# One stage for the attention's finish, the convolutions, the output projection and the second norm of a two-layer hybrid diffusion kernel

## The chip, the cores and the metric

The program runs on one core of one Trainium2 chip, in fp32 throughout. The metric is the device time of one execution in microseconds, as the median of several runs. A core has a matrix engine (TensorE, PE in the rows; its weight loads are PEld), a vector engine (DVE), an activation engine (ACT), GpSimd (POOL), and SyncE (SP), which here only starts transfers. The engines run apart from each other and meet at semaphores. Transfers issued by SP are rows named SPq.

## What is computed

Two layers over 1152 tokens of width 1024: 1024 latent tokens and 128 context tokens. The parts that the change touches are these (the rest is cut):

```python
def _trunk_layer(x, cond, p, ...):
    sh1, sc1, g1, sh2, sc2, g2 = silu(cond) @ w_mod + b_mod       # six rows of 1024, one set per token group
    h = rmsnorm(x, norm_g[0]) * (1 + sc1) + sh1
    z = h @ w_in                                                  # split among three head groups
    o_hg = hgrn(...)                                              # 256 columns
    o_da = rmsnorm(diff_attention(...), diff_subln_g) * (1 - lam_init)      # 4 heads x 128 columns
    zc = short_conv(z_hy, conv_w, conv_b); v, x1, x2 = split(zc)  # Hyena, 3 x 256 columns
    y = x1 * long_conv(v, filt[0]);  o_hy = x2 * long_conv(y, filt[1])
    mix = concat(o_hg, o_da, o_hy) @ w_out
    x = x + g1 * mix
    h2 = rmsnorm(x, norm_g[1]) * (1 + sc2) + sh2
    x = x + g2 * expert_choice_ffn(h2)                            # 16 experts, router on h2
```

## The kernel before

The program is a sequence of stages, each a block in which every engine has its own written-out instruction list. The order within an engine is the order of the code; nothing reorders it. `stage` (L70) opens a block with its own semaphores. At its end all engines meet, SP clears each of the stage's semaphores with one instruction (L83), and all engines meet again (L84) before anything of the next stage starts. Transfers of a stage are therefore issued only after that.

The stages are: `prologue` (L2423), and then for each of the two layers `modulate_and_filter` (L1058), `norm_to_channels` (L87), `project_and_recur` (L219), `attention` (L842), `hyena_and_finish` (L1357), `project_out_and_norm` (L1738) and `route_and_experts` (L1909), and at last `epilogue`.

`prologue` copies the whole input x (4.7 MB) into an internal DRAM tensor `x_rows`, and loads six small constants. The last of these (`select_e`) is issued only when the copy has landed, and the SiLU on ACT waits for all six.

`modulate_and_filter` multiplies the condition by `w_mod` in 12 blocks of 512 columns. `modulate(b)` leaves 4 partial rows in PSUM, ACT keeps them, and `turn(b)` sums and turns them into columns (four pairs of passes of 2 columns each, L1119). Between the blocks PE makes 20 filter spectra of the convolutions, which DVE takes out of PSUM in order (`take`, L1299) into a buffer that SP stores to DRAM (L1107, L1108, L1110). SP's queue carries the `w_mod` blocks and the DFT tables first, then these stores.

`hyena_and_finish` begins with SP loading z0 (the first of six 128-channel blocks of the convolution's input), four small vectors, four DFT units, z1, z2, four more units, z3, z4 and the rest. DVE: `short(0)`, `short(1)` (short convolution of a block; L1590, L1594, L1598), `finish_attention` (row sums of squares L1606, root, scaling of 128x4608 values L1612), `short(2)`, `short(3)`, then `products` and `result` for two orders and two halves `ct`. ACT: the square of the whole attention output (L1559), `centre(1)` (L1540, centre tap of block 1), `take_in(0)` (L1546, L1549, token rows out of PSUM), `centre(2)`, the root, `centre(3)`, `take_in(1)` and so on. PE: `turn_in(0)` (9 transposes, L1422), `forward(0,0)` (L1458, 64 products in 128 passes with 8 DFT units), `turn_in(1)`, `forward(0,1)` with the attention's transposes between, `inverse(0,0)` (L1478), `ctx_forward` (L1497), `inverse(0,1)`, and the same for order 1, ending with `inverse(1,1)`. DVE then does `result(1,1)` (L1661, L1664).

`project_out_and_norm` begins with SP loading `w_out` in two halves of 2 MB (L1751), the router weights (L1752) and the first three token tiles of x (L1758). Meanwhile DVE makes 16 diagonal matrices of the gate g1 (`gate_rows`, L1727), PE multiplies them by ones (L1734) and ACT copies the 2 x 1024 gate rows out of PSUM (L1883). Then for each of 9 token tiles t: PE makes 16 products of 512 columns (32 passes, L1812); DVE multiplies by the gate (L1844) and adds x (L1848); ACT squares (L1890); the norm's row follows; PE transposes the tile before it (L1776), and ACT and DVE shape h. Tile t+1's products are queued on PE ahead of tile t's transposes.

## Time and profile before

| | |
|---|---|
| median of 3 runs | 4454.81 us (4450.07 to 4462.17) |
| the profiled execution | 4453.28 us, of it span 4451.5 us |
| mean granted TensorE clock | 0.951 of full speed |
| PE busy | 3987.0 us (90%), 24498 passes |
| DVE, ACT, POOL busy | 1689.1, 1057.1, 160.3 us |
| DMA | 666.12 MB, mean 150 GB/s |

The span is from the first to the last instruction; the execution's own time is 1.8 us longer. A product in fp32 is two passes on PE, so the rows count passes. PE is busy 90% of the span, but shares of busy time say little here, since the stages follow one another and each has its own limit. What a change in one stage gives is read from the instruction that ends last in it, and from the idle time before the next stage's first instruction.

### The profile page before, as it was taken

How to read it: one execution, taken by the hardware profiler on the slowest of the kernel's cores; microseconds unless marked ns; L12 is line 12 of the kernel's file. 1: busy time of each engine (PE TensorE's matmuls, PEld its weight loads, DVE VectorE, ACT ScalarE, POOL GpSimd, SP SyncE). 2: the span in 40 equal slices, each digit the busy share in tenths (PEclk: the TensorE clock that was granted, in tenths of full speed). 3: DMA queues.
4: the chain of work that ended last, by engine and by line, in shares of the span. 5: the costliest groups of instructions: out<-in, count | busy, mean ns of one | idle time of the engine just before them, and what ended most of it. 6: DMA issues, size and time to landing. Idle time of an engine off the chain costs nothing. (4 is left out here: it accounts for less than half of the span.)

```text
span 4451.5 us, 57780 instructions
## 1 busy us (share of the span) xinstructions
PE 3987.0 (90%) x24498; PEld 3176.2 (71%) x24498; DVE 1689.1 (38%) x2954; ACT 1057.1 (24%) x2386; POOL 160.3 (4%) x96
## 2 busy tenths in 40 slices
PE   6899999787894999999887999988889869999996
PEld 2456885575544999999834668856665369999995
DVE  3335752677535111111142368327774341111111
ACT  1252211673011111111112522117720101111112
POOL 0000002000000000000000000010000000000000
PEclk9899999998996999999988999999989889999998
DMA  6511120103124887788455011210032257787774
GB/s 229 208 37 47 38 68 31 48 1 117 68 90 177 288 283 257 278 284 286 139 205 193 29 56 39 80 54 4 1 117 96 104 214 270 274 288 276 264 273 177
DMA packets 321775, 666.12 MB, mean 150 GB/s; under 512 B 21966, under 2 KB 60494, under 8 KB 319376
## 3 DMA queue, kind: packets, MB, share of 16 engines
q1 hardware_dynamic: 309712, 619.44, 38.3%
q0 software_dynamic: 9216, 33.56, 3.2%
q10 hardware_dynamic: 2592, 9.44, 0.5%
q8 instruction: 195, 3.19, 0.3%
q14 instruction: 60, 0.49, 0.0%
HBM read 596.34 MB, written 70.78 MB: 150 GB/s over the span
## 5 line engine op out<-in xcount | busy, mean ns | idle before, releaser
L2024 PE MATMUL ps<-arena 128*128 128x144 f32 x8192 | 1014.9, 287 | 10.3 <-DVE arena L2184 10.3
L2024 PEld LDWEIGHTS ps<-arena 128*128 128x128 f32 x8192 | 1008.0, 190 | 17.9 <-DVE arena L2184 17.9
L384 PE MATMUL ps<-arena 128*128 128x384 f32 x1920 | 631.0, 490 | 9.4 <-PEq L84 9.4
L384 PEld LDWEIGHTS ps<-arena 128*128 128x128 f32 x1920 | 365.5, 192 | 258.8 <-issue 15.3
L2048 PE MATMUL ps<-arena 128*128 128x144 f32 x4096 | 507.1, 286 | 0.0
L2048 PEld LDWEIGHTS ps<-arena 128*128 128x128 f32 x4096 | 503.6, 190 | 0.0
L2195 DVE TENSOR_TENSOR arena<-arena,ps 128x144 f32<-128x144 f32 x256 | 77.9, 304 | 920.1 <-ACT arena L2100 920.1
L2100 ACT ACTIVATE arena<-ps 128x144 f32<-128x144 f32 x256 | 74.3, 290 | 1011.7 <-PE ps L2024 1011.7
L1812 PE MATMUL ps<-arena 128*128 128x512 f32 x576 | 252.3, 597 | 5.7 <-DMA arena<-in_w_out 5.7
L381 PE MATMUL ps<-arena 128*128 128x256 f32 x1152 | 256.0, 380 | 0.0
L2184 DVE TENSOR_SCALAR arena<-ps,mod 128x128 f32<-128x128 f32 x256 | 87.1, 403 | 435.5 <-PE ps L2004 435.5
L526 ACT ACTIVATE arena<-ps 128x384 f32<-128x384 f32 (+1 forms) x192 | 86.1, 449 | 691.5 <-PE ps L384 463.9
L381 PEld LDWEIGHTS ps<-arena 128*128 128x128 f32 x1152 | 216.5, 191 | 28.4
L2107 ACT ACTIVATE arena<-ps,mod 128x128 f32<-128x128 f32 (+1 forms) x512 | 136.0, 317 | 386.6 <-PE ps L2048 386.6
L1009 ACT ACTIVATE arena<-ps,arena 128x768 f32<-128x768 f32 (+2 forms) x272 | 205.4, 767 | 31.2 <-DVE arena L973 28.9
L1812 PEld LDWEIGHTS ps<-arena 128*128 128x128 f32 x576 | 108.7, 191 | 139.8 <-issue 137.6
L889 PE MATMUL ps<-arena 64*128 64x256 f32 (+2 forms) x1056 | 169.7, 461 | 26.3 <-PEq L84 18.4
L429 PEld LDWEIGHTS ps<-arena 128*128 128x128 f32 x1296 | 158.2, 198 | 29.5 <-issue 23.6
L429 PE MATMUL ps<-arena 128*128 128x128 f32 x1296 | 159.8, 281 | 21.8 <-DVE arena L761 20.8
L938 PE MATMUL ps<-arena 128*128 128x128 f32 x1296 | 169.8, 278 | 1.8 <-ACT arena L1021 1.6
L938 PEld LDWEIGHTS ps<-arena 128*128 128x128 f32 x1296 | 157.3, 194 | 3.4 <-ACT arena L1021 3.1
L918 PE MATMUL ps<-ident,arena 128*128 128x128 f32 x648 | 110.5, 284 | 53.7 <-DVE arena L989 50.2
(307 smaller groups left out, 3887.9 us busy)
## 6 DMA issues: line engine op xcount, KB each, us to landing
arena<-in_w_gate SPq DMA_DIRECT2D x64, 2048.0 KB, 7.9
arena<-in_w_up SPq DMA_DIRECT2D x64, 2048.0 KB, 14.0
arena<-in_w_down SPq DMA_DIRECT2D x64, 2048.0 KB, 12.3
arena<-in_w_mod SPq DMA_DIRECT2D x24, 2048.0 KB, 15.1
arena<-in_w_in SPq DMA_DIRECT2D x28, 1024.0 KB, 5.3
arena<-in_dft_units SPq DMA_DIRECT2D x48, 512.0 KB, 7.2
arena<-x_rows SPq DMA_DIRECT2D x47, 512.0 KB, 6.2
x_rows<-arena ACTq DMA_DIRECT2D x18, 512.0 KB, 2.6
```

The lines of the kernel that those rows point to most:

```text
L381: last = nc.tensor.matmul(m.ps[:, at:at + 256], m.hT[:, k, q * P:(q + 1) * P], m.Wr[:, slot % 2, k, :], start=(k == 0), stop=(k == KD - 1))
L384: last = nc.tensor.matmul(m.ps[:, at:at + TC], m.Wr[:, slot % 2, k, jj * P:(jj + 1) * P], m.hT[:, k, q * TC:(q + 1) * TC], start=(k == 0), ...
L429: last = nc.tensor.matmul(m.ps[:, at:at + P], keys[:, ch * P:(ch + 1) * P], m.xq[:, n % 2, ch].rearrange("p hh t -> p (hh t)"), start=keys ...
L889: last = nc.tensor.matmul(banks[:, mp, col:col + keys.shape[1]], m.aqk[r, h, qt * P:(qt + 1) * P], keys[r], start=True, stop=True)
L918: last = nc.tensor.transpose(m.ps[:, 3072 + k * P:3072 + (k + 1) * P], m.prob[:, n % 2, 0, j * P:(j + 1) * P], m.ident[:, :])
L938: last = nc.tensor.matmul(m.ps[:, 3584:3584 + DV], m.aT[:, n % 2, j, :], v, start=(j == 0), stop=(j == nk - 1))
L1009: nc.scalar.activation(m.prob[:, n % 2, mp, a:b], banks[:, mp, 0:b - a], ACT.Exp, bias=m.nmax[:, n, mp:mp + 1], accum_out=m.sums[:, n, int ...
L1812: last = nc.tensor.matmul(m.ps[:, at:at + 512], m.oT[:, k, t * P:(t + 1) * P], m.wo[:, k, h * 512:(h + 1) * 512], start=(k == 0), stop=(k ...
L2024: last = nc.tensor.matmul(m.ps[:, at:at + CAP], m.wbuf[:, 2 * h + which, k, q * P:(q + 1) * P], m.xe[:, e % 2, k, :], start=(k == 0), stop ...
L2048: last = nc.tensor.matmul(m.ps[:, at:at + CAP], m.wbuf[:, 4 + h, k, q * P:(q + 1) * P], m.hid[:, k, :], start=(k == 0), stop=(k == KD - 1))
L2107: last = nc.scalar.activation(m.yT[:, n, a:b], m.ps[:, at + a:at + b], ACT.Copy, scale=m.mod[:, 5 * KD + n, g:g + 1])
L2184: last = nc.vector.tensor_scalar(m.xe[:, e % 2, k, 0:CAP_L], m.ps[:, 3072 + k * P:3072 + (k + 1) * P], m.mod[:, 4 * KD + k, 0:1], m.mod[:, ...
```

## The change

The stages `hyena_and_finish` and `project_out_and_norm` become one, `mix_and_norm`. The attention stage loads z0 to z2 and the four small vectors (with one new semaphore). In the merged stage ACT's square stands behind `take_in(0)`. SP issues the two halves of `w_out` once all forward transforms are through, into the place of the forward DFT units; the gate rows and three tiles of x follow once all products are through. PE starts tile 0 of the projection with 14 of its 16 products right behind `inverse(1,1)`; the last two wait for `result(1,1)`. `gate_rows` is gone. In its place the modulation stage turns blocks 4 and 5, which hold g1, with one product of 16 x 512 each, DVE adds the bias to 2 x 512 values twice, and SP stores the rows to DRAM (four new semaphores). The input x is no longer copied: layer 0 reads it where it lies.

```diff
--- before.py
+++ after.py
...
-                sp.dma_start(xbuf[:, t], m.x_dram[t * P:(t + 1) * P, :]).then_inc(s[f"x_loaded{t}"], 16)
+                sp.dma_start(xbuf[:, t], m.x_in(l)[t * P:(t + 1) * P, :]).then_inc(s[f"x_loaded{t}"], 16)
...
+            for j in range(3):
+                sp.dma_start(m.z[j], m.zhy_dram[j * P:(j + 1) * P, :]).then_inc(s["z_loaded"], 16)
+            for dst, src in ((m.hy_cw, "hy_conv_w"), (m.hy_cb, "hy_conv_b"), (m.hy_skip, "hy_skip"),
+                             (m.sub_gain, "diff_subln_col")):
+                sp.dma_start(dst[:, :], m.d[src][l]).then_inc(s["z_loaded"], 16)
             sp.wait_ge(s["spectra_loaded"], 80)
+            sp.wait_ge(s["z_loaded"], 112)
...
+            sp.wait_ge(s["w_used"], 8)
+            sp.dma_start(m.gate_bias[:, :], m.d["gate_bias"][l]).then_inc(s["gate_bias"], 16)
+            sp.wait_ge(s["gate_rows"], 2)
+            for i in range(2):
+                sp.dma_start(m.gate_dram[:, i * PC:(i + 1) * PC], m.gate_rows[32 * i:32 * i + 2, :])\
+                    .then_inc(s["gate_stored"], 16)
...
+            sp.wait_ge(s["gate_stored"], 32)
...
+                if b in GATE_BLOCKS:
+                    i = 32 * (b - GATE_BLOCKS[0])
+                    if i == 0:
+                        pe.wait_ge(s["sums_read"], 1)
+                    nc.tensor.matmul(m.ps[i:i + E, 2560:3072], m.select_e[:, :], m.mod_rows[:, b % 2, :], start=True,
+                                     stop=True).then_inc(s["turned"], 1)
+                    return
...
+                if src == 2560:
+                    dve.sem_inc(s["sums_read"], 1)
...
+            dve.wait_ge(s["gate_bias"], 16)
+            dve.wait_ge(s["turned"], 6)
+            for i in range(2):
+                r = slice(32 * i, 32 * i + 2)
+                nc.vector.tensor_tensor(m.gate_rows[r, :], m.ps[r, 2560:3072], m.gate_bias[r, :], ALU.add)\
+                    .then_inc(s["gate_rows"], 1)
...
-def hyena_and_finish(nc, m, l):
+def mix_and_norm(nc, m, l):
...
-            load_z(0)
-            for dst, src in ((m.hy_cw, "hy_conv_w"), (m.hy_cb, "hy_conv_b"), (m.hy_skip, "hy_skip"),
-                             (m.sub_gain, "diff_subln_col")):
-                sp.dma_start(dst[:, :], m.d[src][l]).then_inc(s["w_loaded"], 16)
...
-            load_z(1)
-            load_z(2)
...
+            sp.wait_ge(s["forward"], 8)
+            w = m.d["w_out"][l].rearrange("(k p) (h n) -> h p k n", p=P, n=512)
+            for h in range(2):
+                sp.dma_start(m.wo[:, :, h * 512:(h + 1) * 512], w[h]).then_inc(s[f"w_loaded{h}"], 16)
+            sp.wait_ge(s["spectra"], 8)
+            for g in range(2):
+                sp.dma_start(m.gbo[:, g], m.gate_dram[g].partition_broadcast(P)).then_inc(s["gate_loaded"], 16)
...
+                    if t == 3:
+                        sp.wait_ge(s["result"], 8)
+                        sp.dma_start(m.wr[:, :, :], m.d["w_router"][l]).then_inc(s["router_loaded"], 16)
...
+            for t in range(NT):
+                if t >= 2:
+                    pe.wait_ge(s["scaled"], t - 1)
+                if t == 0:
+                    pe.wait_ge(s["result"], 6)
+                    for h in range(2):
+                        pe.wait_ge(s[f"w_loaded{h}"], 16)
+                        project(t, h, range(KD - 1))
+                    pe.wait_ge(s["result"], 8)
+                if t == 1:
+                    pe.wait_ge(s["ctx_result"], 8)
+                for h in range(2):
+                    last = project(t, h, range(KD) if t else range(KD - 1, KD))
+                last.then_inc(s["projected"], 1)
...
-            nc.scalar.activation(sq, m.o_att.rearrange("p c v -> p (c v)"), ACT.Square).then_inc(s["square"], 1)
-            act.wait_ge(s["w_loaded"], 64)
             centre(1)
             take_in(0)
+            nc.scalar.activation(sq, m.o_att.rearrange("p c v -> p (c v)"), ACT.Square).then_inc(s["square"], 1)
...
-                    dve.wait_ge(s["z0"], 16)
...
-            dve.wait_ge(s["w_loaded"], 64)
...
-def gate_rows(nc, m, block_engines, s, which):
...
-def project_out_and_norm(nc, m, l):
...
-            gate_rows(nc, m, (dve, None), s, 0)
-            dve.wait_ge(s["rows_ready"], 1)
+            dve.wait_ge(s["gate_loaded"], 32)
...
-            act.wait_ge(s["diag_used"], 16)
-            nc.scalar.activation(m.gbo.rearrange("p g n -> p (g n)"), m.ps[:, 2048:4096], ACT.Copy)\
-                .then_inc(s["rows_ready"], 1)
...
-        m.wo = view(m.R_W, KD, D)
-        m.xr = view(9216, 3, D)
-        m.dx = view(12288, 2, D)
...
+        m.wo = view(38656, KD, D)
+        m.xr = view(25088, 3, D)
+        m.dx = view(28160, 2, D)
...
-        m.gbo = view(19456, 2, D)
+        m.gbo = view(47908, 2, D)
...
+        m.x_in = lambda l: m.x_dram if l else d["x"]
+        m.gate_dram = nc.dram_tensor("mix_gate", (2, D), F32, kind="Internal").ap()
...
-            hyena_and_finish(nc, m, l)
-            project_out_and_norm(nc, m, l)
+            mix_and_norm(nc, m, l)
...
-    with stage(nc, m, "loaded", "copied", "silu") as (block, s):
+    with stage(nc, m, "loaded") as (block, s):
         @block.sync
         def _(sp):
-            sp.dma_start(m.x_dram, m.d["x"]).then_inc(s["copied"], 16)
             sp.dma_start(m.cond[:, :, :], m.d["cond"]).then_inc(s["loaded"], 16)
             sp.dma_start(m.row_number[:, :], m.d["row_number"]).then_inc(s["loaded"], 16)
             sp.dma_start(m.ident[:, :], m.d["ident"]).then_inc(s["loaded"], 16)
             sp.dma_start(m.select[:, :], m.d["select"]).then_inc(s["loaded"], 16)
             sp.dma_start(m.alt[:, :], m.d["alt"]).then_inc(s["loaded"], 16)
-            sp.wait_ge(s["copied"], 16)
             sp.dma_start(m.select_e[:, :], m.d["select_e"]).then_inc(s["loaded"], 16)
             sp.wait_ge(s["loaded"], 96)
```

The first place is the start of the stage on ACT, in layer 0. The 128x4608 row is the attention's square, the 128x1152 rows are `centre`, and 128x8x128 with 128x128 is `take_in(0)`. Before:

```order
L1559 ACTIVATE arena<-arena 128x4608
L1540 ACTIVATE arena<-arena,hy_cb,hy_cw 128x1152
L1546 ACTIVATE arena<-ps 128x8x128
L1549 ACTIVATE arena<-ps 128x128
L1540 ACTIVATE arena<-arena,hy_cb,hy_cw 128x1152
L1565 ACT_TABLE_LOAD
L1565 ACTIVATE small<-small 128x36
```

After:

```order
L1657 ACTIVATE arena<-arena,hy_cb,hy_cw 128x1152
L1663 ACTIVATE arena<-ps 128x8x128
L1666 ACTIVATE arena<-ps 128x128
L1678 ACTIVATE arena<-arena 128x4608
L1657 ACTIVATE arena<-arena,hy_cb,hy_cw 128x1152
L1681 ACT_TABLE_LOAD
L1681 ACTIVATE small<-small 128x36
```

The square has moved from the first place to the fourth, behind the two copies that release PE's first transform; the root (128x36) keeps its place.

The second place is PE at the seam of the two old stages, layer 0: the last inverse transforms, the gate rows (`ones`), and the projection (128x512 of L1812). Here rows count products, not passes. Before:

```order
L1506 MATMUL ps<-arena 128x128 x4
L1478 MATMUL ps<-arena 128x512 x16
L76 UNCONDITIONAL_BRANCH
L1766 UNCONDITIONAL_BRANCH
L1734 MATMUL ps<-arena,ones 128x128 x16
L1812 MATMUL ps<-arena 128x512 x32
L1776 MATMUL ps<-ident,arena 128x128 x8
```

After:

```order
L1557 MATMUL ps<-arena 128x128 x4
L1529 MATMUL ps<-arena 128x512 x16
L1623 MATMUL ps<-arena 128x512 x32
L1594 MATMUL ps<-ident,arena 128x128 x8
```

The two branches (the end of one stage and the start of the next) and the 16 products with `ones` are gone, and the projection's 32 products of tiles 0 and 1 stand directly behind the last inverse.

The third place is SP around the old seam. Before, with the 48 semaphore clears between the stages (ISA) and the 29 at the second stage's end further down:

```order
L1412 DMA arena<-in_dft_units 128x1024 x8
L1390 DMA arena<-z_hyena 128x1152
L76 UNCONDITIONAL_BRANCH
L83 ISA x48
L1747 UNCONDITIONAL_BRANCH
L1751 DMA arena<-in_w_out 128x8x512 x2
L1752 DMA arena<-in_w_router 128x256
...
L83 ISA x29
```

After, with the clears of the merged stage at its end:

```order
L1440 DMA arena<-in_dft_units 128x1024 x8
L1424 DMA arena<-z_hyena 128x1152
L1446 DMA arena<-in_w_out 128x8x512 x2
L1449 DMA arena<-mix_gate 128x1024 x2
L1458 DMA arena<-in_x 128x1024 x3
...
L1454 DMA arena<-in_w_router 128x256
...
L83 ISA x71
```

The loads of `w_out` now stand behind the last convolution input in the same queue, and 48 + 29 clears at two ends have become 71 at one. The same count is 34 before and 38 after at the modulation stage's end, 13 and 14 at the attention's, and 3 and 1 at the prologue's.

## Rows read from the trace of the kernel before

**Rows 1.** Timeline of the prologue: start, length, engine, line; then idle time before.

```profile
0.74 0.65 SPq L2428 DMA_DIRECT2D x_rows<-in_x  x1
...
3.90 0.49 SPq L2433 DMA_DIRECT2D alt_sb<-in_alt  x1
17.76 0.33 SPq L2435 DMA_DIRECT2D select_e_sb<-in_select_e  x1
...
20.36 0.37 SPq L1075 DMA_DIRECT2D arena<-in_pos_all  x1
```

**Rows 2.** Landing of the four small vectors (L1395), layer 0.

```profile
DMA to landing us min/median/max: 2.7/3.1/3.6
```

**Rows 3.** Timeline of the convolution stage's start, layer 0.

```profile
1027.59 4.04 ACT L1559 ACTIVATE arena<-arena 128x4608 f32<-128x4608 f32 x1 [1.24 <-PEq L84]
...
1033.03 0.88 DVE L1590 TENSOR_SCALAR arena<-arena,hy_cw,hy_cb 128x1152 f32<-128x1152 f32 x1 [8.85 <-DMA sub_gain<-in_diff_subln_col]
...
1037.13 2.19 PE L1422 MATMUL ps<-ident,arena 128*128 128x128 f32 x9 [11.19 <-DVE arena L1598]
...
1040.98 1.00 ACT L1546 ACTIVATE arena<-ps 128x1024 f32<-128x1024 f32 x1
...
1042.04 1.34 ACT L1540 ACTIVATE arena<-arena,hy_cb,hy_cw 128x1152 f32<-128x1152 f32 x1
...
1042.25 17.41 PE L1458 MATMUL ps<-arena 128*128 128x128 f32 x128 [2.93 <-ACT arena L1546]
...
1044.15 4.94 DVE L1606 TENSOR_REDUCE small<-arena 128x36 f32<-128x4608 f32 x1
```

**Rows 4.** The same stage, later: PE waits for DVE; a later forward transform.

```profile
1100.07 2.07 PE L1497 MATMUL ps<-arena 128*128 128x256 f32 x4 [2.76 <-DVE arena L1652]
...
1119.28 14.56 PE L1458 MATMUL ps<-arena 128*128 128x128 f32 x128 [1.11 <-ACT arena L1555]
```

**Rows 5.** Busy time in one stretch; last three: granted clock, DMA share, GB/s.

```profile
1034.00:1036.00 2.00, 0.00 (x0) 0.00 (x0) 1.97 (x3) 0.00 (x0) 0.00 (x0) 0.50 1.01 397
```

**Rows 6.** The convolution stage's start, layer 1.

```profile
3229.11 4.04 ACT L1559 ACTIVATE arena<-arena 128x4608 f32<-128x4608 f32 x1 [1.22 <-PEq L84]
...
3245.61 4.95 DVE L1606 TENSOR_REDUCE small<-arena 128x36 f32<-128x4608 f32 x1
```

**Rows 7.** Timeline of the seam, layer 0, and one steady tile.

```profile
1182.10 1.28 DVE L1661 SCALAR_TENSOR_TENSOR arena<-arena,hy_sk,ps 128x1024 f32<-128x1024 f32 x1 [4.67 <-PE ps L1478]
...
1188.23 1.01 SPq L1751 DMA_DIRECT2D arena<-in_w_out  x2
...
1197.57 29.40 PE L1812 MATMUL ps<-arena 128*128 128x512 f32 x64 [3.67 <-DMA arena<-in_w_out]
...
1213.35 1.22 DVE L1844 TENSOR_TENSOR arena<-ps,arena 128x1024 f32<-128x1024 f32 x1 [20.03 <-PE ps L1812]
...
1227.68 13.90 PE L1812 MATMUL ps<-arena 128*128 128x512 f32 x32
```

**Rows 8.** The seam, layer 1.

```profile
3383.63 1.28 DVE L1661 SCALAR_TENSOR_TENSOR arena<-arena,hy_sk,ps 128x1024 f32<-128x1024 f32 x1 [4.67 <-PE ps L1478]
...
3411.37 1.22 DVE L1844 TENSOR_TENSOR arena<-ps,arena 128x1024 f32<-128x1024 f32 x1 [16.73 <-PE ps L1812]
```

**Rows 9.** The semaphore clears of L83 between 1180 and 1200 us.

```profile
L83 SPq EVENT_SEMAPHORE_RANGE_CLEAR  x48: 25/25/31, 1184.9 to 1187.9; - x48
```

**Rows 10.** Timeline of the modulation stage's last part, layer 0.

```profile
151.45 1.06 SPq L1090 DMA_DIRECT2D arena<-in_w_mod  x2
...
163.53 0.95 PE L1119 MATMUL ps<-select_sb,arena 128*128 128x2 f32 x8
...
170.00 0.69 DVE L1299 TENSOR_TENSOR arena<-ps,arena 128x512 f32<-128x512 f32 x1 [5.58 <-PE ps L1200]
...
190.77 0.32 SPq L1110 DMA_DIRECT2D filter_spectra<-arena  x1
```

**Rows 11.** Landing of the last two `w_mod` loads (L1090), layer 0.

```profile
DMA to landing us min/median/max: 9.5/11.9/14.4
```

More of the change, by code:

```diff
@@ L1065, in modulate_and_filter @@
     G = KD // 4
-    with stage(nc, m, *(f"w_loaded{b}" for b in range(NBUF)), "w_used", "mod_small", "cond_ready", "rows_kept", "turned", "step",
+    GATE_BLOCKS = (4, 5)
+    with stage(nc, m, *(f"w_loaded{b}" for b in range(NBUF)), "w_used", "sums_read", "gate_bias", "gate_rows", "gate_stored", "mod_small", "cond_ready", "rows_kept", "turned", "step",
                "small_loaded", "decay_loaded", "biased", "hidden", "argued", "reduced", "sine", "taps_done", "taps",
@@ L1535, in _ @@
+            turn_x(NT - 1)
+            router(2)
+            turn_logits(2)
         @block.scalar
@@ L2401, in build @@
         m.ctx_table = view(51712, 2, CTX)
+        m.gate_bias, m.gate_rows = view(34304, 512), view(34816, 512)
         m.cond32 = view(51968, KD, 32)
```

245 lines of the change are left out of this document (105 added, 140 removed).

## The prediction

> **What bounds the kernel now.** I read the page's table by engine first, then the timeline at each place that the diff touches, and asked there which instruction ends last. PE is busy 90% of the span, so time can come only from stretches in which PE stands still, and there are three. The prologue: nothing computes until the copy of x has landed, since the last small load is issued behind it, at 17.76 us, and the next stage's first transfer goes out at 20.36 [rows 1]. The start of the convolution stage: ACT starts at 1027.59, but DVE only at 1033.03, when the small vectors and z0 are there, and PE at 1037.13 after 11.19 us idle [rows 3]. The seam: PE's last inverse releases DVE at 1182.10, and DVE gets the first projected tile at 1213.35, 31.25 us later, although a steady tile is 13.90 us of PE [rows 7]. In layer 1 the same stretch is 3383.63 to 3411.37, 27.74 us [rows 8]. Within the stages I look for who waits: at 1100.07 PE resumes after 2.76 us idle, released by DVE [rows 4], so up to there DVE's chain of products sets the time, and what the stage's start gives is what it gives DVE, not PE.
>
> **Prologue.** The copy's issue, the first on SP (at 0.74, 0.65 long), goes, and the small loads move up by about 0.7 us: `alt` from 3.90 to 3.2, and `select_e`, whose wait is gone, 0.5 behind it to 3.7. Before, from that issue to the next stage's first transfer were 20.36 - 17.76 = 2.60 us, landing, SiLU and clears included; kept, the next stage starts at 6.3, a gain of 14.1 [rows 1]. Six small loads now land together. The four small vectors, issued side by side behind one big load, took 2.7 to 3.6 us to land [rows 2], which would be up to 1.9 worse: 12.2. I take 13.6, near the first end, because here no big load is among them. Two clears fewer give 0.1, inside the rounding. From there layer 0's modulation runs as before, since its loads are issued by the start of the stage, and x is read later at the same size from another place.
>
> The Trainium skill ("DMA: Bandwidth & Descriptors", the anatomy of one DMA) gives a fixed part of about 2.0 us and a rate of 436 GB/s; for the 64 KB identity that is an estimate of 2.15 us, and the prologue's gain would be 13.6 to 13.7.
>
> **Start of the convolution stage.** z0, z1 and z2 (each 128x1152 values, 1.8 MB together) and the vectors come in during attention, a stage in which SP has only the spectra to load at its start; at 397 GB/s [rows 5] they are 4.5 us of transfer beside all of attention's compute. So DVE starts `short(0)` with the stage. From its start to PE's transposes were 1037.13 - 1033.03 = 4.10 us; the transposes take 2.19; `take_in(0)` on ACT 1042.04 - 1040.98 = 1.06; then the square, which stands there now, 4.04 [rows 3]. 4.10 + 2.19 + 1.06 + 4.04 and 0.1 of hand-overs are 11.5 us from stage start to DVE's row sums, where before it was 1044.15 - 1027.59 = 16.56. That is 5.05 us, and layer 1 repeats it: 3245.61 - 3229.11 = 16.50 [rows 6]. `short(1)` and `centre(1)` fit in before the square ends. PE's first transform starts 4.10 + 2.19 + (1042.25 - 1040.98) = 7.6 us into the stage, before 14.7, so PE gains 7.0, but 2 us of these turn into waiting for DVE: the idle of 2.76 [rows 4] becomes about 4.8. The move of the square is what makes the two differ. DVE sits idle some 4 us before the row sums now. The DFT units: z1 and z2 are no longer between them. At 397 GB/s [rows 5] one unit of 0.52 MB takes 1.3 us, and PE uses one in 17.41 / 8 = 2.2 us, the first only 7.6 us into the stage, so no transform waits. Gain 2 x 5.05 = 10.1.
>
> The clock is a loss here. The granted clock in rows 5 is 0.50, the lower level (1.2 GHz), after PE had been idle; the transform that began then took 17.41 us against 14.56 for the same work at full clock [rows 3, 4]. After the idle of 2.76 the four short passes took 2.07 us, at the lower level too. A longer idle may lengthen that stretch: from 0 (the 2.76 us row already paid) to 2.85 (the difference 17.41 - 14.56) per layer. I take 0.7, since the row at the same place is nearest: minus 1.4 in all. The Trainium skill ("TensorE: Matmul & The Clock Gate", why this matters for your kernels) says that an idle gap between bursts of matmuls drops PE to its lower clock and that sustained work brings it back. By that rule a gap that already drops the clock costs no more when it grows, and the sum would be 1.4 better.
>
> **The seam.** Gone are the 48 clears, which took 3.0 us from 1184.9 to 1187.9 [rows 9], the gate rows, ACT's copy, and the wait for `w_out`, which ended last in layer 0 at 1197.57 [rows 7]. After, PE goes from the last inverse straight into 28 of tile 0's 32 passes: 28 x 13.90 / 32 = 12.2 us. In that time DVE does `result(1,1)`, 2.5 us, so the last four passes do not wait. Tile 0 ends 13.9 us after the inverse. Gains: 31.25 - 13.9 = 17.35 and 27.74 - 13.9 = 13.85, together 31.2. The difference of the two was the clock and the landing, and neither is left. What could be late is `w_out`: SP issues it when the last forward transform is done, and two inverse transforms of 32 such passes, 27.8 us at least, lie between that and tile 0; 2 x 2 MB loads in another stage took up to 14.4 to land [rows 11]. Behind it in the queue stand the two gate loads of 0.5 MB and three tiles of x, 2.5 MB together, issued after DVE's last product, which the second half of the last inverse needs, so 7 us or more before its end, and needed 13.9 after it: 21 us for 6.3 us at 397 GB/s. Nothing waits. The router's weights come after `result(1,1)` and are read at tile 4, 60 us on.
>
> **What comes back.** The clears are serial: 3.0 / 48 = 0.0625 us each [rows 9]. The merged stage ends with 71 instead of 29, so 42 x 0.0625 = 2.6 us per layer, all on the path, 5.25 in all. Four more at each modulation stage and one at each attention stage: 10 x 0.0625 = 0.6.
>
> **Modulation.** On PE, block 4 and 5 are turned by 2 passes of 512 columns, 2 x 0.43 = 0.87 us, in place of 8 short ones of together 0.95 [rows 10]: nothing. `sums_read` is given right behind a row sum's reciprocal that DVE does before the first spectrum, and asked after the second lot of spectra. The two additions of 2x512 out of PSUM stand on DVE behind the take at 170.00 and cost about 0.7 each (the take of 128x512 is 0.69, a bound from above). Behind them are two tiny rows, the first `edge` and four more takes; DVE has slack until 190.77, where the last store is released by the last take [rows 10]. The first two stores go out 1.4 later, with some 19 us left to the last one's issue. The bias load is issued at 152.5, behind two `w_mod` loads that land at most 14.4 later, at 166.3 [rows 10, 11]; needed at 170.7. So the cost is nothing, from above bounded by 1.4 per layer if DVE's slack were gone, and not below nothing, since no work on PE goes.
>
> **The sum**, against the profiled execution: 13.6 + 10.1 - 1.4 + 31.2 - 5.25 - 0.6 = 47.65. 4453.28 - 47.65 = 4405.6 us. The median shown is 1.5 us above that execution, so I forecast 4406.
>
> **Rivals.** *A, the transfers take the place of the wait at the start.* Eight units go out at once when the stage opens. If the first transform ran at their pace, all of the 10.1 would be lost: 4416. Against it stands the 397 GB/s. *B, the seam gives only the clears and the gate rows.* If `w_out` lands so late that tile 0 still waits for it, as it does at 1197.57 in layer 0, the seam gives about half, 15.6: 4422. It needs a landing of over 28 us. *C, slower.* The bias load stands in one queue with the `w_mod` loads, and DVE waits for it in front of takes 16 to 19, which release PE's banks and the spectra's stores. If it lands at T after 170.7, DVE's slack is used up first (20 us to the last store's issue, less 5 of its own work and some 5 that the stores would come late: I take 10), then each us is lost twice, once per layer. Against a gain of 47.65 it decides from T = 170.7 + 10 + 24 = 205 us, 52 us after issue, against 14.4 seen; at 60 us (T = 212) it is 2 x 31 - 47.65 = 14 over, 4468. *D, the copy was hidden anyway*, that is, layer 0's modulation is bound by its `w_mod` stream from the first load on and only the start moves: the stream moves too, as it is issued by that start, so I give this little; it would cost 13.6: 4419. *E, the clock rule above*: 4404, inside my own range.
>
> **Chances.** Forecast with E 0.82 (4397 to 4413 alone: the prologue's 12.2 to 14.1, the clock's 0 to 5.7, about 3 us per start for where the clock rises, and the spread of the runs shown). A 0.06, B 0.03, D 0.04, C 0.02, nothing gained for another reason 0.03. The range goes from 4396 to 4420, which takes in A and D. A difference of 0.3%, 13.4 us, is about what a measurement of this kernel can tell from none. All cases but C and the last are faster by more: 0.95 faster, 0.03 within, 0.02 slower.
>
> **What would show it.** Right: the modulation stage's first transfer at 6 to 8 us; DVE's row sums 11 to 12 us after the stage's start, with ACT's square as their releaser; PE idle 4 to 6 us before the first context transform and DVE named for it; no idle on PE between the last inverse and tile 0, DVE's first gate multiplication 14 us after its `result(1,1)` starts; 71 clears over 4.4 us at the merged stage's end; DVE not waiting for a transfer behind take 15. Wrong: a wait for `in_w_out`, `in_dft_units` or `mix_gate` on any engine, PE at the lower clock in tile 0, or a first transform that starts later than 9 us into the stage.

## The result and the profile after

| | before | after |
|---|---|---|
| median | 4457.95 us (4450.07 to 4462.17, 4 runs) | 4408.41 us (4401.24 to 4408.75, 4 runs) |
| profiled execution | 4453.28 us, span 4451.5 | 4408.75 us, span 4407.0 |
| mean granted TensorE clock | 0.951 | 0.95 |

The ratio is 0.9889, with a 95% interval from 0.9876 to 0.9901. The forecast was 4406 us, inside 4396 to 4420. Between the two profiled executions lie 44.5 us, against a sum of 47.65; between the medians lie 49.5.

Prologue, layer 0, from the timeline (start, length, engine, line, then the idle time before it and what ended it). It answers to [rows 1].

```profile
3.07 0.43 SPq L2430 DMA_DIRECT2D select_e_sb<-in_select_e  x1
4.92 0.22 ACT L2440 ACTIVATE cond<-cond 128x16 f32<-128x16 f32 x1 [2.90 <-DMA select_e_sb<-in_select_e]
5.71 0.37 SPq L1082 DMA_DIRECT2D arena<-in_pos_all  x1
```

The last small load goes out at 3.07 instead of 17.76. From it to the next stage's first transfer are 2.64 us, as against 2.60 before. The start has moved by 20.36 - 5.71 = 14.65 us.

The merged stage's start, layer 0, the same view. It answers to [rows 3].

```profile
1014.27 1.35 ACT L1657 ACTIVATE arena<-arena,hy_cb,hy_cw 128x1152 f32<-128x1152 f32 x1 [1.29 <-PEq L84]
1014.29 0.88 DVE L1740 TENSOR_SCALAR arena<-arena,hy_cw,hy_cb 128x1152 f32<-128x1152 f32 x1 [3.78 <-PEq L84]
...
1018.39 1.79 PEld L1473 LDWEIGHTS ps<-ident,arena 128*128 128x128 f32 x9 [6.11 <-DVE arena L1748]
...
1020.62 1.02 ACT L1663 ACTIVATE arena<-ps 128x1024 f32<-128x1024 f32 x1 [5.01 <-PE ps L1473]
...
1021.70 4.04 ACT L1678 ACTIVATE arena<-arena 128x4608 f32<-128x4608 f32 x1
...
1021.91 6.36 PE L1509 MATMUL ps<-arena 128*128 128x128 f32 x32 [1.33 <-ACT arena L1663]
...
1025.78 4.95 DVE L1756 TENSOR_REDUCE small<-arena 128x36 f32<-128x4608 f32 x1 [4.41 <-ACT arena L1678]
```

DVE begins with the stage, its row sums (L1756) start 11.51 us later and wait for the square (4.41 us idle, released by L1678). In [rows 3] it was 16.56. Look also at ACT in front of 1020.62: it has stood idle for 5.01 us, waiting for PE's transposes, and the square of 4.04 us is only started behind them.

PE in the rest of that stage, layer 0. It answers to [rows 4] and to the last inverse.

```profile
1081.70 1.93 PE L1548 MATMUL ps<-arena 128*128 128x256 f32 x4 [5.06 <-DVE arena L1802]
1083.42 14.83 PE L1529 MATMUL ps<-arena 128*128 128x512 f32 x32
...
1149.98 15.70 PE L1529 MATMUL ps<-arena 128*128 128x512 f32 x32 [1.87 <-DVE arena L1802]
```

PE waits 5.06 us for DVE in front of the first context transform, as forecast (4 to 6). The last row was not forecast: the last inverse takes 15.70 us. In the kernel before, the same passes with the same idle time in front of them took 14.00:

```profile
1168.06 14.00 PE L1478 MATMUL ps<-arena 128*128 128x512 f32 x32 [1.88 <-DVE arena L1652]
```

The granted clock in and behind the first passes of this inverse shows why (busy time of each engine in a stretch; the last three columns are the granted clock, the DMA share and GB/s). The first two rows are of the changed kernel, the third is of the kernel before:

```profile
1150.00:1153.00 3.00, 3.00 (x4) 1.36 (x5) 2.90 (x6) 0.00 (x0) 0.00 (x0) 0.53 0.00 0
1154.00:1157.00 3.00, 3.00 (x9) 1.33 (x8) 2.86 (x5) 0.00 (x0) 0.00 (x0) 1.00 0.17 37
1168.50:1171.50 3.00, 3.00 (x8) 1.33 (x7) 2.90 (x7) 0.00 (x0) 0.00 (x0) 1.00 0.00 0
```

The seam, layer 0, then layer 1. They answer to [rows 7, 8].

```profile
1165.72 1.28 DVE L1811 SCALAR_TENSOR_TENSOR arena<-arena,hy_sk,ps 128x1024 f32<-128x1024 f32 x1 [6.37 <-PE ps L1529]
...
1179.52 1.22 DVE L1880 TENSOR_TENSOR arena<-ps,arena 128x1024 f32<-128x1024 f32 x1 [11.26 <-PE ps L1623]
```

```profile
3350.00 1.28 DVE L1811 SCALAR_TENSOR_TENSOR arena<-arena,hy_sk,ps 128x1024 f32<-128x1024 f32 x1 [6.37 <-PE ps L1529]
...
3363.80 1.22 DVE L1880 TENSOR_TENSOR arena<-ps,arena 128x1024 f32<-128x1024 f32 x1 [11.26 <-PE ps L1623]
```

PE's first product of tile 0 starts at 1165.51, without idle time in front. DVE's first gate multiplication comes 13.80 us after `result(1,1)` starts, in both layers, where it was 31.25 and 27.74. The two halves of `w_out` had been issued from 1132.65 on and landed at most 13.0 us later. No engine waits for it, nor for the gate rows.

The clears at the merged stage's end, layer 0. They answer to [rows 9].

```profile
L83 SPq EVENT_SEMAPHORE_RANGE_CLEAR  x71: 25/25/30, 1315.1 to 1319.0; - x71
```

71 clears take 3.8 us in layer 0, 0.055 each, and 4.2 in layer 1, 0.060 each. The 29 of the old second stage had taken 1.5 in either layer (layer 1: 3547.0 to 3548.5), so the end is 2.3 and 2.7 us longer.

The modulation stage, DVE and then SP, layer 0. It answers to [rows 10].

```profile
154.85 0.69 DVE L1322 TENSOR_TENSOR arena<-ps,arena 128x512 f32<-128x512 f32 x1 [5.58 <-PE ps L1221]
155.46 1.38 DVE L1354 TENSOR_TENSOR arena<-ps,arena 2x512 f32<-2x512 f32 x2
```

```profile
137.40 4.57 SPq L1113 DMA_DIRECT2D arena<-in_gate_bias  x1
...
158.30 0.35 SPq L1120 DMA_DIRECT2D filter_spectra<-arena  x1
158.69 0.43 SPq L1121 DMA_DIRECT2D filter_spectra<-arena  x1
175.63 0.32 SPq L1123 DMA_DIRECT2D filter_spectra<-arena  x1
```

The two additions follow the take at 154.85 without waiting. The last store goes out 15.14 us earlier than at 190.77, which is the prologue's shift.

### The profile page after: what moved, and what is told of

It reads as the page before. It is cut to its first block and busy times, and to the rows that moved or that the text cites. A ratio compares the mean times of both kernels' runs of the same rounds, so it can differ in the third digit from the quotient of the medians.

```text
span 4407.0 us, 57543 instructions
## 1 busy us (share of the span) xinstructions
PE 3977.7 (90%) x24410; PEld 3164.0 (72%) x24410; DVE 1684.2 (38%) x2928; ACT 1054.5 (24%) x2384; POOL 160.4 (4%) x96
```

## The experiments

Ten kernels: the changed kernel once more, and nine edits of it. "Stage length" below is from the end of the stage before (its last clear) to the end of this one, read from where the clears lie. The same stage of the changed kernel is 305.00 and 305.77 us long (layers 0 and 1) in the first profile.

**The changed kernel again.**

> The changed kernel itself, once more, so that the others can be held against it on the same chip. Both theories: a median of 4404 to 4410, 42 to 54 us under the kernel before; in its trace the same steps as in the first one: row sums 11.5 us after the merged stage starts, PE idle 5.06 us before the first context transform, 13.8 us from result(1,1) to the first gate multiplication. If the 15.7 us of the last inverse (14.0 before) come from where the clock happens to change, this row may differ here; if they come from the code, it is 15.7 again.

4408.92 us (4406.08 to 4412.77), ratio to before 0.9894 [0.9876, 0.9911]. PE's last inverse, layer 0, and the clock in its first passes:

```profile
1154.18 14.00 PE L1529 MATMUL ps<-arena 128*128 128x512 f32 x32 [1.89 <-DVE arena L1802]
```

```profile
1154.50:1157.50 3.00, 3.00 (x8) 1.33 (x7) 2.90 (x6) 0.00 (x0) 0.00 (x0) 1.00 0.00 0
```

Same program, same idle in front (1.89), but 14.00 us at full clock; layer 1 has 14.00 too. So the 1.7 us per layer are not in the code. The merged stages are 303.30 and 303.63 long here, which is 1.7 and 2.1 less.

**The square back in front of the copies.**

```diff
             centre(1)
-            take_in(0)
             nc.scalar.activation(sq, m.o_att.rearrange("p c v -> p (c v)"), ACT.Square).then_inc(s["square"], 1)
+            take_in(0)
```

> ACT's square of the attention output stands between centre(1) and take_in(0) instead of behind take_in(0). Theory (the square on ACT bounds DVE's chain, and ACT is idle 5.01 us in front of take_in(0)): the square runs from 1.35 to 5.4 us after the stage's start, take_in(0) starts at 6.35 as now, DVE's row sums start about 7.1 instead of 11.5 us after the stage's start, PE's idle before the first context transform falls from 5.06 to about 0.7, and each layer gains 4.4: about 4399.5; up to 1.8 per layer more, 4396, if the lower clock behind that idle goes with it. Rival 1 (PE's transforms bound the stretch, or what DVE gains is waited out at a later meeting): the row sums move, the end does not, 4408. Rival 2 (take_in(0) is pushed back by the square): PE's first transform later than 7.65 us after the start, 4408 to 4412.

4393.0 us (4392.52 to 4396.09), ratio to before 0.9859 [0.9842, 0.9876], 15.9 under the changed kernel on the same chip. The start, layer 0, and PE at the context transform:

```profile
1013.35 1.35 ACT L1657 ACTIVATE arena<-arena,hy_cb,hy_cw 128x1152 f32<-128x1152 f32 x1 [1.29 <-PEq L84]
...
1014.61 4.03 ACT L1677 ACTIVATE arena<-arena 128x4608 f32<-128x4608 f32 x1
...
1017.48 2.20 PE L1473 MATMUL ps<-ident,arena 128*128 128x128 f32 x9 [5.82 <-DVE arena L1748]
...
1019.71 1.02 ACT L1663 ACTIVATE arena<-ps 128x1024 f32<-128x1024 f32 x1 [1.08 <-PE ps L1473]
...
1020.37 4.94 DVE L1756 TENSOR_REDUCE small<-arena 128x36 f32<-128x4608 f32 x1
```

```profile
1076.33 1.13 PE L1548 MATMUL ps<-arena 128*128 128x256 f32 x4 [0.68 <-DVE arena L1802]
1077.30 13.90 PE L1529 MATMUL ps<-arena 128*128 128x512 f32 x32
```

The square fills ACT's idle time, `take_in(0)` still starts 6.36 us into the stage, and the row sums start at 7.02 in place of 11.51. PE's idle is 0.68, and the four passes and the inverse behind them take 1.13 and 13.90, at full clock. The merged stages are 297.17 and 297.54 long, 6.1 less than in the repeat: 4.5 of DVE's chain and 1.7 of the clock behind the idle. That is 12.2 for both, and the theory's mechanism holds; both rivals fall. The time came out 3 us below the theory's lowest (4396): the other 3.7 of the medians' difference are not the square's as far as the profiles show. Between these two they lie in stages that are the same, above all the projection of layer 1 (558.05 against 560.64).

**The start as before.**

```diff
-            for j in range(3):
-                sp.dma_start(m.z[j], m.zhy_dram[j * P:(j + 1) * P, :]).then_inc(s["z_loaded"], 16)
...
-            sp.wait_ge(s["z_loaded"], 112)
...
+            load_z(0)
+            for dst, src in ((m.hy_cw, "hy_conv_w"), (m.hy_cb, "hy_conv_b"), (m.hy_skip, "hy_skip"),
+                             (m.sub_gain, "diff_subln_col")):
+                sp.dma_start(dst[:, :], m.d[src][l]).then_inc(s["vectors"], 16)
             for u in range(4):
...
+            load_z(1)
+            load_z(2)
             for u in range(4, 8):
...
+            nc.scalar.activation(sq, m.o_att.rearrange("p c v -> p (c v)"), ACT.Square).then_inc(s["square"], 1)
+            act.wait_ge(s["vectors"], 64)
             centre(1)
             take_in(0)
-            nc.scalar.activation(sq, m.o_att.rearrange("p c v -> p (c v)"), ACT.Square).then_inc(s["square"], 1)
```

> The start of the merged stage is undone: z0, z1, z2 and the four vectors are loaded at its start again, in the old order, and the square is ACT's first instruction. The rest of the change stays. Theory: DVE's row sums 16.5 us after the stage's start, PE's idle before the first context transform 2.8 us, each layer 5.05 us longer: 4408.4 + 10.1 = 4418.5. Rival (loads of 1.8 MB in attention cost that stage what they save here, since attention was 0.7 and 2.6 us longer after than before): attention back at 238.4 and 236.9 us, 4415. If attention's lengths are a matter of where the clock falls, they stay anywhere in 236.9 to 239.5.

4418.92 us (4414.06 to 4421.7), ratio to before 0.9912 [0.9897, 0.9927], 10.0 over the repeat. Layer 0's start:

```profile
1013.62 4.04 ACT L1675 ACTIVATE arena<-arena 128x4608 f32<-128x4608 f32 x1 [1.22 <-PEq L84]
...
1018.90 0.88 DVE L1741 TENSOR_SCALAR arena<-arena,hy_cw,hy_cb 128x1152 f32<-128x1152 f32 x1 [8.77 <-DMA sub_gain<-in_diff_subln_col]
...
1030.63 4.95 DVE L1757 TENSOR_REDUCE small<-arena 128x36 f32<-128x4608 f32 x1
```

The row sums come 17.0 us after the start, and 16.2 in layer 1, against 11.5: together 10.2, so the forecast's 10.1 is there. PE's idle time before the first context transform is 3.12 and 4.06. The merged stages are 5.8 and 6.7 longer than in the repeat, 12.5 in all, of which 3.4 are the last inverses at the lower clock again (15.70 in both layers).

Attention is 237.57 and 236.64 us, shorter than the 239.08 and 239.48 of the changed kernel, as the rival wanted; but the last experiment below, which has the loads, shows 236.98 and 237.14. The difference is in PE's clock some 222 us into the stage. The same four passes, behind the same idle time, in the repeat and then here:

```profile
1000.97 1.11 PE L924 MATMUL ps<-ident,arena 128*128 128x128 f32 x4 [1.53 <-ACT arena L1027]
```

```profile
997.77 0.66 PE L918 MATMUL ps<-ident,arena 128*128 128x128 f32 x4 [1.53 <-ACT arena L1021]
```

Over all profiles the clock falls there in 17 of 20 layers that have the loads, and in 1 of 4 that do not (the kernel before and this one); the means are 238.6 and 237.4. Where it does not fall, attention is 236.98 to 237.14 long with the loads and 236.64 to 237.57 without. So the loads do not lengthen attention's own work. Whether they bring the fall, and with it the 1.2 us between the means, is open: four layers without them are too few.

**The copy back.**

```diff
+            sp.dma_start(m.x_dram, m.d["x"]).then_inc(s["copied"], 16)
...
+            sp.wait_ge(s["copied"], 16)
             sp.dma_start(m.select_e[:, :], m.d["select_e"]).then_inc(s["loaded"], 16)
...
-        m.x_in = lambda l: m.x_dram if l else d["x"]
+        m.x_in = lambda l: m.x_dram
```

> The copy of x and the wait for it are put back into the prologue, and layer 0 reads the copy. Theory: all of it is serial, the next stage's first transfer goes from 5.7 to 20.4 us, and nothing of it is made good: 4408.4 + 14.7 = 4423.1. Rival (layer 0's modulation is bound by its stream of weights, so the prologue's time was hidden): 4408 to 4412, the stage's end moving by less than 4 us.

4420.06 us (4417.0 to 4427.27), ratio to before 0.9918 [0.9902, 0.9934]. The prologue:

```profile
18.29 0.33 SPq L2432 DMA_DIRECT2D select_e_sb<-in_select_e  x1
...
20.81 0.37 SPq L1082 DMA_DIRECT2D arena<-in_pos_all  x1
```

The next stage starts 15.1 us later, and the modulation stage ends at 196.41 in place of 182.53, 13.9 later. Of the 14.7 the medians show 11.1: the modulation stage is 175.91 us long here and 177.16 and 181.84 in the two profiles of the changed kernel, and its passes, the same in all three, take PE 147.3 us here against 148.1 and 153.0. The copy was not hidden.

**Two stages again, loads early.**

```diff
...
+               "ctx_turned", "w_loaded0", "w_loaded1", "gate_loaded", "x_early") as (block, s):
...
+            for t in range(3):
+                sp.dma_start(m.xr[:, t], m.x_in(l)[t * P:(t + 1) * P, :]).then_inc(s["x_early"], 16)
+            for h in range(2):
+                sp.wait_ge(s[f"w_loaded{h}"], 16)
+            sp.wait_ge(s["gate_loaded"], 32)
+            sp.wait_ge(s["x_early"], 48)
...
+    with stage(nc, m, "x_loaded0", "x_loaded1", "x_loaded2",
...
```

The first block ends with these waits on SP and, on the other engines, with what stands before the projection; the second holds the rest.

> The merged stage is cut in two again at the seam; w_out, the gate rows and the first three tiles of x are still loaded early, in the first of the two, and there are no gate products. Theory (stage end and wait for transfers are two separate parts of the seam): the stage's end costs what it did before from DVE's release to SP's first issue, 6.1 us; the clock is lower behind it, so tile 0 takes about 15.7: from result(1,1) to the first gate multiplication 21.9 us in place of 13.8. Per layer 8.1 lost, some 2.4 of clears moved to this place and so given back at the end: 5.7 each, 4408.9 + 11.4 = 4420. Rival 1 (the stage's end is nearly all of the seam): 28 to 31 us at the seam, 4437 to 4443. Rival 2 (the stage's end is nothing once the loads are early): 16 us or less, 4409 to 4412.

4421.46 us (4420.74 to 4422.12), ratio to before 0.9921 [0.9904, 0.9938], 12.5 over the changed kernel. The seam, layer 0:

```profile
1164.67 1.28 DVE L1699 SCALAR_TENSOR_TENSOR arena<-arena,hy_sk,ps 128x1024 f32<-128x1024 f32 x1 [6.37 <-PE ps L1517]
...
1170.40 19.93 PE L1813 MATMUL ps<-arena 128*128 128x512 f32 x39 [5.77 <-PEq L84]
...
1187.36 1.23 DVE L1890 TENSOR_TENSOR arena<-ps,arena 128x1024 f32<-128x1024 f32 x1 [20.15 <-PE ps L1813]
```

PE is idle for 5.77 us and then begins tile 0 at the lower clock (0.50 up to 1176, 1.00 from 1178 on). It is 22.69 us from `result(1,1)` to the gate multiplication, 8.9 more than in one stage, and 23.03 in layer 1, 9.2 more. The merged stages' work is 6.4 us longer per layer than in the first profile. So the stage's end, with the clock behind it and the passes that start before `result(1,1)` is through, costs 8.9 us of the 17.45 gained at layer 0's seam, and 8.6 stay without joining the stages.

**`w_out` late.**

```diff
-            sp.wait_ge(s["forward"], 8)
+            sp.wait_ge(s["result"], 8)
             w = m.d["w_out"][l].rearrange("(k p) (h n) -> h p k n", p=P, n=512)
             for h in range(2):
                 sp.dma_start(m.wo[:, :, h * 512:(h + 1) * 512], w[h]).then_inc(s[f"w_loaded{h}"], 16)
-            sp.wait_ge(s["spectra"], 8)
```

> SP issues w_out, the gate rows and x only when DVE is through with result(1,1); everything else as in the changed kernel, one stage. Theory: PE stands still behind the last inverse until about 9.3 us after the issue of w_out, as in the kernel before, so about 12 us, and tile 0 then takes about 15.8: the first gate multiplication comes 28 us after result(1,1) starts in place of 13.8, 4408.9 + 28 = 4437. It would show that without the early load most of the seam's gain is lost though the stage's end is gone. Rival (the stage's end and the gate rows were the seam, the load lands in time all the same): 14 to 18 us at the seam, 4409 to 4417.

4434.07 us (4432.91 to 4436.21), ratio to before 0.995 [0.9933, 0.9967]. The seam, layer 0:

```profile
1161.65 1.28 DVE L1810 SCALAR_TENSOR_TENSOR arena<-arena,hy_sk,ps 128x1024 f32<-128x1024 f32 x1 [4.67 <-PE ps L1528]
...
1164.22 1.10 SPq L1446 DMA_DIRECT2D arena<-in_w_out  x2
...
1172.78 27.48 PE L1622 MATMUL ps<-arena 128*128 128x512 f32 x57 [11.16 <-DMA arena<-in_w_out]
...
1189.63 1.23 DVE L1879 TENSOR_TENSOR arena<-ps,arena 128x1024 f32<-128x1024 f32 x1 [25.44 <-PE ps L1622]
```

PE waits 11.16 us for the transfer, 28.0 from `result(1,1)` to the gate multiplication, as expected to a tenth, and 27.0 in layer 1. The stages are 12.5 and 13.2 longer than in the first profile, the time 25.2 longer than in the repeat. With the stage's end gone but the load late, 3.3 of layer 0's 17.45 are left and 0.7 of layer 1's 13.94; with the load early but the stages apart, 8.6 and 4.7 (the experiment before). So the early load is worth something by itself, and joining the stages almost nothing without it. The two losses add up to more than the gain (8.9 + 14.2 against 17.45), since each of the two kernels pays for DVE's `result(1,1)` (2.5 us) and for the lower clock behind PE's idle time (about 3 us on the passes of tiles 0 and 1), and with both parts undone these would be paid once.

**One clear for a range.**

```diff
-        for s in sems.values():
-            nc.sync.sem_clear(s)
+        nums = sorted(s.num for s in sems.values())
+        runs = []
+        for n in nums:
+            if runs and runs[-1][1] == n:
+                runs[-1][1] = n + 1
+            else:
+                runs.append([n, n + 1])
+        for a, b in runs:
+            nc.sync.sem_clear(range(a, b))
```

> Each stage clears its semaphores with one instruction over their range of numbers (three where the range has gaps) in place of one instruction for each. Theory (the price is one of the instruction, 0.055 us each: 3.9 us for the merged stage's 71): 525 instructions become about 20, so 505 x 0.055 = 28 us go, 4381, and from the merged stage's last clear to the next stage's first instruction stays what it is. Rival 1 (the price is one of the semaphore, whatever instruction clears it): 4409. Rival 2 (the clears lie beside something else at most stage ends): the gain between 0 and 28, the stages' ends showing which.

4379.27 us (4378.75 to 4380.81), ratio to before 0.9827 [0.9811, 0.9843], 29.6 under the changed kernel. The clears of the merged stage, and the largest single one (64 semaphores, in place of 3.5 us):

```profile
L90 SPq EVENT_SEMAPHORE_RANGE_CLEAR  x3: 53/60/89, 1306.2 to 1306.4; - x3
```

```profile
L90 SPq EVENT_SEMAPHORE_RANGE_CLEAR  x1: 133/133/133, 765.7 to 765.7; - x1
```

30 instructions are left of 525, and the price is almost all the instruction's: 0.133 us for 64 semaphores. At 0.055 to 0.060 each the 495 gone are 27.2 to 29.7 us, and in the first profile of the changed kernel the clears took 29.9 us from first to last, summed over all stages' ends. The place where it shows is the gap between two stages: from DVE's last instruction in `project_and_recur` to PE's first in attention it is 2.3 us now (763.78 to 766.11) and 6.2 in the changed kernel (768.98 to 775.21).

**DVE loaded behind take 15.**

```diff
                 r = slice(32 * i, 32 * i + 2)
+                for _ in range(10):
+                    c.then_wait(dve, nc.vector.tensor_tensor(m.gate_rows[r, :], m.ps[r, 2560:3072], m.gate_bias[r, :], ALU.add))
                 nc.vector.tensor_tensor(m.gate_rows[r, :], m.ps[r, 2560:3072], m.gate_bias[r, :], ALU.add)\
                     .then_inc(s["gate_rows"], 1)
```

> Behind take 15 in the modulation stage DVE does each of the two gate-row additions ten times more before the one that counts, 20 more of 2x512, each waiting for the one before it, about 15 us of DVE more per layer at the place that rival C spoke of. By the prediction's slack (DVE not needed until the last store's issue, of which it allowed 10 us): 15 - 10 = 5 us per layer, 4419. By the changed kernel's trace another bound comes first: the store issued at 158.7 lands 13.8 us later, at 172.5, and the last store lands at 179.5, so only 7 us are free and the stage's end moves by 15 - 7 = 8 per layer: 4408.9 + 16 = 4425. If DVE's place were bound: 15 per layer, 4439.

4422.53 us (4419.75 to 4425.6), ratio to before 0.9922 [0.9905, 0.9938]. SP in layer 0's modulation:

```profile
172.12 0.35 SPq L1120 DMA_DIRECT2D filter_spectra<-arena  x1
172.51 0.43 SPq L1121 DMA_DIRECT2D filter_spectra<-arena  x1
175.28 0.32 SPq L1123 DMA_DIRECT2D filter_spectra<-arena  x1
```

The last store (L1123) is issued on time, so DVE had the slack. But the stores before it go out 13.8 late; the one issued at 172.51 lands 12.0 later and is still under way beside it. The last store takes 11.7 us to land where it took 3.8, and lands at 187.0 instead of 179.4. The stage is 184.78 and 184.87 us long, 7.6 and 8.2 more than in the first profile of the changed kernel. The two times ten additions took 14.2 us, so the slack at this place is 6 to 7 us, and it ends at a landing, not at an issue.

**The square and the ranges together.**

```diff
-        for s in sems.values():
-            nc.sync.sem_clear(s)
+        for a, b in runs:
+            nc.sync.sem_clear(range(a, b))
...
             centre(1)
-            take_in(0)
             nc.scalar.activation(sq, m.o_att.rearrange("p c v -> p (c v)"), ACT.Square).then_inc(s["square"], 1)
+            take_in(0)
```

> The edits of the square (between centre(1) and take_in(0)) and of the clears (one per range) together. Theory (they lie at different places and do not meet): 4393.0 and 4379.3 were 15.9 and 29.6 under the changed kernel's 4408.9, so 45.5 together: 4363.4. Of the square's 15.9 its own profile shows only 2 x 6.1 to 2 x 8 in the merged stages, the rest lying where the clock fell elsewhere, so 4363 to 4367 is the theory. Rival (a part of either gain was the clock's and is not had twice): 4367 to 4375.

4369.12 us (4366.19 to 4369.57), ratio to before 0.9807 [0.9794, 0.9821]. It is the fastest, 1.9% under the kernel before, but 2 us above the theory, in the rival's range. The merged stages are 293.60 and 293.63 long, 8.2 less than with the ranges alone: the 4.5 of DVE's chain, and 3.7 of clock, behind both idle times. PE at the context transform, layer 0:

```profile
1069.05 1.13 PE L1555 MATMUL ps<-arena 128*128 128x256 f32 x4 [0.33 <-DVE arena L1809]
```

So the edits add where they work: 16.5 us by the two stages. The medians show 10.2 against the ranges alone (measured on another chip), since the stages that both kernels have alike are 3.9 longer in this profile (such as modulation, 173.93 against 172.99), and the two spans differ by 12.6. The rival is right in this: of the square's 15.9 us, the 3.7 that lay in other stages were not its own.

**The idle time filled.**

```diff
+            for _ in range(2):
+                ctx_inverse(1, False)
             ctx_inverse(1)
             inverse(1, 1)
```

With `False` it does the same passes and signals nothing.

> The changed kernel, with ctx_inverse(1) done three times in place of once (16 passes of 128x128 more, about 2.1 us), in the 1.87 us in which PE waits for DVE in front of the last inverse. Theory (it is this idle behind which the granted clock falls in some executions, and the last inverse then takes 15.7 in place of 14.0): no lower clock at this place in either layer, the last inverse 13.9 to 14.0 in both, its start 0.2 to 0.5 later; the time 4405 to 4409. Rival (the clock there does not hang on the idle): 15.7 in one layer or both, 4409 to 4410.

4403.93 us (4403.06 to 4404.81), ratio to before 0.9887 [0.9871, 0.9902]. PE there, layer 0:

```profile
1145.64 2.84 PE L1557 MATMUL ps<-arena 128*128 128x128 f32 x24
1148.57 14.00 PE L1529 MATMUL ps<-arena 128*128 128x512 f32 x32
```

Only 0.1 us of idle time is left, the inverse takes 14.00 in both layers, and it starts where it would have. But this does not prove the link. With the 1.9 us of idle time, 13 of 22 last inverses began at the lower clock over all profiles: 11 of 14 in kernels with the square in its changed place (none of the repeat's two), both with the start as before, and none of 6 in the kernel before and in the two with the square put back. Two filled ones without a fall could be chance, and the merged stages are as long as in the repeat (303.25 and 303.66 against 303.30 and 303.63). What the rows do show is that the fall needs more than this idle time, since the same program had it and did not have it. That the time is 1 us better than expected is within what the other stages vary.

## Why the prediction was right, and where its terms were off

| term | predicted | profiled |
|---|---|---|
| prologue | 13.6 | 14.65 |
| start of the convolution stage | 10.1 | 10.0 (5.05 and 4.99) |
| clock behind the context transform's idle time | -1.4 | -0.9 |
| clock in the last inverse | none | -3.4 (0 in the repeat) |
| seam | 31.2 | 31.4 (17.45 and 13.94) |
| clears at the merged stage's end | -5.25 | -5.0 (2.3 and 2.7) |
| attention, with the loads in it | none | -3.3 (0.7 and 2.6) |
| ten more clears, and all other stages | -0.6 | 1.0 |
| sum | 47.65 | 44.5, as measured |

The mechanisms that carry the gain, the prologue, the start and the seam, came as described, 56.1 us of 54.9 predicted. That the sum is only 3 us off is in part luck: two losses that the prediction did not have, 3.4 in the last inverses and 3.3 in attention, stand against 3.5 by which the other terms came out better. In the repeat the first of the two losses was nothing, and its median was 46.3 us under the kernel before.

*Prologue.* The step was right, and rival D is refuted by the copy put back. I was 1 us short. Of this 0.6 is that `select_e` goes out at 3.07 and not at 3.7: with the big copy gone, the issues behind it are shorter too (`ident` 0.43 us; 0.85 with the copy back). The rest is what I took off for slower landings. The six loads did not get in each other's way: ACT's SiLU starts 1.85 us after the last issue. The Trainium skill's fixed part of about 2.0 us ("DMA: Bandwidth & Descriptors", anatomy of one DMA) is near this, though it is given there for transfers issued by GpSimd, and SP issues these; the estimate of 13.6 to 13.7 for the whole prologue is 1 below the trace.

*Start.* Every part of the chain held (4.10, 2.20, 1.08, 4.04), 11.51 us in both layers, and rival A fell: no transform waited for a unit. What the step did not ask is whether the square has to stand in this chain at all. I had the 4 us of DVE's idle time in my text, and took the place of the square as given; that ACT waits 5.01 us in front of `take_in(0)` could have been worked out from [rows 3]. It is worth 4.5 us per layer, and 6.1 with the clock behind the context transform's idle time; the 8.2 against the ranges alone have 1.7 of the last inverse in them, which the repeat shows can be had with the square in either place.

*Clock.* This term was mis-sized, by place more than by price. At the context transform the longer idle time cost 0.3 and 0.6 more than before (17.28 against 16.98 us from that transform to the transposes behind the next inverse in layer 0, 17.68 against 17.05 in layer 1), so rival E was nearly right: a gap that already drops the clock costs little more when it grows. Of the idle times in all profiles, those of 0.3 to 0.7 us in front of this transform never lowered the clock (0 of 4), those of 2.70 to 4.06 did in 3 of 4, those of 4.75 to 6.27 in all 16. The Trainium skill ("TensorE: Matmul & The Clock Gate", why this matters for your kernels) says that gaps between bursts drop the clock; these rows agree, and add that behind a gap of 1.9 us it falls or does not fall in the same program. I had read the row at the last inverse in the kernel before as a fact of that place (14.00), when it was one of two outcomes.

*Attention.* The prediction set the loads' 4.5 us of transfer beside attention's compute and put their effect at nothing. In the first profile attention is 0.7 and 2.6 us longer (layers 0 and 1) than in the kernel before. The length of its own work is the same with the loads and without; a fall of the clock near its end is what differs, and whether the loads bring it stays open (see the start as before).

*Seam.* The forecast of 13.9 us was met with 13.80 in both layers, and rival B fell: `w_out` lands 19 us before it is needed. The two experiments split the term, which I had left whole: putting the stage's end back costs 8.9 us of layer 0's 17.45, and a late load alone costs 14.2.

*Clears.* 0.055 us each in layer 0 and 0.060 in layer 1 instead of 0.0625. The step was right, but I took this price as one of the semaphore. It is one of the instruction.

*Modulation.* The cost is nothing, as said, and rival C had a margin: the bias lands at 151.8 (issued 137.40, 14.4 later), DVE asks for it at 155.5. But the slack that I put at 10 us of DVE is 6 to 7, since the landing of the big store ends first.

## What to carry to other kernels

When a change moves an operation, ask for the idle time of its own engine at the old place, the new one and each between; here the square had a free place of 5 us in front of the copy, and went behind it. A stage's end costs its clears, the lower clock after it and the transfers that may not start before it, and joining two stages paid here only because those transfers were issued early as well; issued early, they gave half of the gain in layer 0 without the joining. What is cheap per piece and repeated in every stage is worth one experiment: one clear per range gave more than half of what the whole change gave.

## What the runs showed of the hardware

- A clear of one semaphore takes 0.055 to 0.065 us of SP where 29 to 71 follow each other, of a range of 64 semaphores 0.133 us in all.
- Behind an idle time of 1.87 to 1.89 us in front of the last inverse, the granted clock was at the lower of its two levels (1.2 of 2.4 GHz) in 13 of 22 profiled layers and at the upper in the others, also of the same program. The price is 1.7 us each time. The runs do not settle what decides it. A like fall near the end of attention (239 against 237 us) came in 18 of 24 layers.
- The modulation stage of one and the same kernel was 177.16 us long in one profile and 181.84 in the next, with PE busy for 148.1 and 153.0 us of it on the same passes. The stage's mean granted clock does not tell the two apart by itself: it was 0.91 and 0.87, and in layer 1 of the second profile 0.87 as well, with 174.4 us. These 4.7 us are about the size of the clears' term, and this is why the trace's own rows decide on a term here and the medians only on the sum.
- A transfer's issue on SP is not of one length: `ident` took 0.43 us, and 0.85 in the kernel with the big copy issued before it.
